# The scan stage of a hybrid decoder trunk: ScalarE in place of VectorE copies the corner product of each inverse out of PSUM

## What is computed

```
def step(state, inp):
    rt, wt, kt, vt, kkt, at = inp
    sa = jnp.einsum('bhij,bhj->bhi', state, -kkt)
    state = (state * wt[:, :, None, :] + sa[..., None] * (kkt * at)[:, :, None, :]
             + vt[..., None] * kt[:, :, None, :])
    return state, jnp.einsum('bhij,bhj->bhi', state, rt)
```

## Time and profile before

| | us |
|---|---|
| median of 3 runs | 3130.48 |
| lowest and highest | 3129.78 and 3132.05 |
| the profiled execution | 3130.32 |
| its span in the trace | 3128.5 |

### The profile page before, as it was taken

How to read it: one execution, slowest core, us unless ns; L and a number is a source line. 1 busy time by engine, 2 the same in 40 slices (tenths; PEclk the granted TensorE clock), 3 DMA queues, 4 the chain that set the end, 5 groups by cost and what they waited for, 6 DMA issues and landing times. The chain is left out here.

```text
span 3128.5 us, 52347 instructions
## 1 busy us (share of the span) xinstructions
PE 3056.2 (98%) x21306; PEld 2537.1 (81%) x21306; DVE 2147.3 (69%) x3225; ACT 1334.0 (43%) x2110; POOL 436.2 (14%) x570
## 2 busy tenths in 40 slices
PE   8999999899999999999999999999999999999998
PEld 6778777788988888778888788888888887888887
DVE  6777685677765677445444777777877777787786
ACT  6757566555545221033333333333433333444443
POOL 4334342655510011000000000000000000000000
PEclk9999999999999999999999999999999999999999
DMA  6466554322101644311111433333333334777873
GB/s 216 148 189 195 168 183 135 106 71 83 64 26 55 229 159 154 117 41 61 67 61 56 145 116 112 111 108 128 119 115 117 108 135 142 254 223 214 252 220 121
DMA packets 200092, 416.43 MB, mean 133 GB/s; under 512 B 15296, under 2 KB 99648, under 8 KB 193600
## 3 DMA queue, kind: packets, MB, share of 16 engines
q1 hardware_dynamic: 199872, 413.34, 39.9%
HBM read 295.82 MB, written 117.46 MB: 132 GB/s over the span
## 5 line engine op out<-in xcount | busy, mean ns | idle before, releaser
L3202 PE MATMUL ffn_ps<-ffn_t_p,ffn_w_p 128*128 128x512 f32 x2640 | 606.1, 389 | 0.0
L3202 PEld LDWEIGHTS ffn_ps<-ffn_t_p,ffn_w_p 128*128 128x128 f32 x2640 | 495.3, 188 | 103.4 <-DVE ffn_w_p L3377 0.6
L3217 PE MATMUL ffn_ps<-ffn_t_p_parts 128*128 128x512 f32 x1416 | 330.7, 393 | 5.8 <-DVE ffn_t_p_parts L3519 5.8
L3217 PEld LDWEIGHTS ffn_ps<-ffn_t_p_parts 128*128 128x128 f32 x1416 | 268.9, 190 | 62.8 <-DVE ffn_t_p_parts L3519 6.6
L431 POOL TENSOR_TENSOR w_low<-w_ring,w_high 128x1024 fp32r<-128x1024 f32 x84 | 215.2, 2564 | 313.1 <-ACT w_high L586 313.1
L3228 ACT ACTIVATE ffn_w_p<-ffn_w_p_sums 128x512 fp32r<-128x512 f32 x132 | 83.4, 632 | 335.7 <-DVE ffn_w_p_sums L3398 335.4
L547 PE MATMUL proj<-hn_high,w_high 128*128 128x512 f32 x544 | 222.0, 416 | 1.7 <-ACT hn_high L576 1.6
L547 PE MATMUL proj<-hn_high,w_low 128*128 128x512 f32 x544 | 209.6, 394 | 0.0
L547 PE MATMUL proj<-hn_low,w_high 128*128 128x512 f32 x544 | 207.9, 391 | 0.0
L3217 PE MATMUL ffn_ps<-ffn_t_p 128*128 128x512 f32 x696 | 162.5, 389 | 0.0
L3298 ACT ACTIVATE ffn_t_p_parts<-ffn_ring 128x1536 fp32r<-128x1536 f32 x59 | 87.7, 1487 | 159.9 <-PE ffn_ps L3217 156.3
(11 more groups left out here) (577 smaller groups left out, 6673.3 us busy)
## 6 DMA issues: line engine op xcount, KB each, us to landing
ffn_ring<-in_w_up SPq DMA_DIRECT2D x44, 1024.0 KB, 5.3
ffn_ring<-in_w_down SPq DMA_DIRECT2D x88, 512.0 KB, 5.4
w_ring<-in_w_feat SPq DMA_DIRECT2D x84, 512.0 KB, 4.0
ffn_ring<-scratch_values SPq DMA_DIRECT2D x88, 257.0 KB, 4.5
scratch_gates<-ffn_gate SPq DMA_DIRECT2D x44, 512.0 KB, 2.6
ffn_ring<-scratch_gates SPq DMA_DIRECT2D x88, 256.0 KB, 3.8
scratch_values<-ffn_raw SPq DMA_DIRECT2D x22, 513.0 KB, 3.5
scratch_values<-ffn_raw SPq DMA_DIRECT2D x22, 512.0 KB, 3.4
```

The lines of the kernel that those rows point to most:

```text
L3202: mm = pe.matmul(bank(name, s), w_part(name, a)[:, k * P:(k + 1) * P], t_part(name, b)[:, k * TB:(k + 1) * TB], start=k == a == b == 0, st ...
L3217: mm = pe.matmul(ps[:, DOWN_BANKS[2 * t + c]], down_part(n, x)[:, HID + t * TC:HID + (t + 1) * TC], down_part(n, y)[:, c * DH:(c + 1) * DH ...
```

## The change

The copy `corner_products(n)` moves from VectorE's queue to ScalarE's. In an iteration with a late chunk, VectorE goes from `prepare_kr` directly to `corner_scores(n)`. ScalarE does the copy after `level_out(m, 1)` and before `corner_inverse_out(n)`. What it reads and writes, and the semaphores that it waits for and signals, are the same; the form of the instruction on ScalarE is an activation with the function Copy.

```
@@ in the queue of ScalarE
+            def corner_products(n):
+                act.wait_ge(*cy_done.at(n))
+                act.activation(corner_y[HD:].rearrange("p h n -> p (h n)"), ps_g[HD:, n % 2, SIDES[0]], ACT.Copy).then_inc(cy_out.sem, 1)
+
             def corner_inverse_out(n):
                 act.wait_ge(*cx_done.at(n))
@@ its run(i)
                 if early:
                     level_out(m, 1)
                 if late:
+                    corner_products(n)
                     corner_inverse_out(n)
                     diagonal(n, 0, inv_out)
@@ in the queue of VectorE
-            def corner_products(n):
-                dve.wait_ge(*cy_done.at(n))
-                dve.tensor_copy(corner_y[HD:].rearrange("p h n -> p (h n)"), ps_g[HD:, n % 2, SIDES[0]]).then_inc(cy_out.sem, 1)
@@ its run(i)
                 if late:
-                    corner_products(n)
                     corner_scores(n)
                     picks_last(n)
```

## The result

| | before | changed |
|---|---|---|
| median, us | 3130.97 | 3137.88 |
| lowest and highest | 3127.52 and 3136.06 | 3134.75 and 3140.57 |
| runs | 18 | 18 |
| the profiled execution | 3130.32 | 3136.44 |
| its span | 3128.5 | 3134.7 |

The changed kernel is 0.19% slower by the ratio in the table, 5.9 us with an interval of 4 to 8; the two medians of the table lie 6.9 us apart. The forecast was 3133.6 us in a range of 3130.2 to 3136.0: the direction was right, the time lies outside the range. Single runs of either kernel spread over 6 to 9 us, so times are compared over many runs.

The account below looks back on a forecast made before the run. The prediction took TensorE's own queue as the bound of a usual iteration. Lateness of 14 x 0.20 = 2.8, plus 0.05 and 0.33, made 3.2 us, on 3130.4 giving 3133.6 us, range 3130.2 to 3136.0.

Parts of the forecast that it names:

- TensorE's queue sets the pace, VectorE waits: Usual iteration of the scan, 20.9 us: TensorE's own queue bounds it, VectorE waits before the copy, its relief gains nothing.
- The rival of VectorE's relief: Where TensorE waits for `kc`, each wait shrinks by 0.46 us, 2.8 us in six, giving 3130.8 us; chance 0.04.
- The copy takes 0.38 us, the release 0.05: Corner copy on ScalarE: length 0.38 us, as L1260, then 0.05 us from its end to the start of `corner_inverse`.
- It starts 0.50 us after `level_out`: ScalarE, usual chunk: corner copy overlaps `level_out`, starting 0.50 us after its start, so TensorE waits 0.20 us.
- no overlap at all: High end for a usual chunk: corner copy starts only when `level_out` (0.62 us) ends, making `corner_inverse` 0.32 us late.
- The last chunk, 0.48 us after `oy`: Last chunk, without `level_out`: copy starts 0.48 us after `oy`, `corner_inverse` is 0.58 us late, `rhs` 0.33 us later.
- The delay passes on 1:1: After `corner_inverse`: `off_times` and all later waits move with the delay, so each chunk's 0.20 us counts in full.
- the absorbed rival: In the scan, the delay meets waits that start elsewhere: 0 to 1 us, 3130.4 to 3131.4 us; chance 0.12.
- The sum: Over the scan's 16 chunks: 14 x 0.20 = 2.8, plus 0.05 for chunk 0 and 0.33 for the last, 3.2 us.
- The slower rival: Before `corner_inverse`: no overlap, 0.32 us, plus a TensorE restart of 0.14 a chunk, 7.0 us, 3137.4 us; chance 0.09.
- The clock: TensorE's half-clock dip after a long wait: one dip removed or added, at most 1.7 us, 3131.9 or 3135.3; chance 0.07.

Follow-up runs that it names:

- the wide copy: The changed kernel with ScalarE's corner copy over all 128 partitions in place of 64 to 127: 3133.72 us, 1.0006 of the kernel before.

## Why the prediction was wrong

- **TensorE's queue sets the pace, VectorE waits.** Right at the place of the change, not everywhere. VectorE's idle time before `factor` went from 0.39 to 1.11 us, forecast about 1, and nothing came back from its 16 missing copies. The rival of VectorE's relief falls: TensorE's six waits for `kc` went from 6.1 us only to 5.7. But "no matmul waits for a result of VectorE" was read off a list that can't show such a wait under matmuls still counted as busy: in every usual chunk L1614 was held up by VectorE's `start_inverse`, by up to 0.17 us. It follows the wait for `off_times`, so the lateness still passed through, and the relief could not reach it.
- **The copy takes 0.38 us, the release 0.05.** Right, 0.379 and 0.05. The corner copy on ScalarE is the shorter one (0.38 against 0.43 us), and it made no gain, since its place outweighed it.
- **It starts 0.50 us after `level_out`.** This is the step that failed. It took 0.64. The overlaps used were those between copies that all begin at partition 0; the corner copy begins at partition 64. The bound "no overlap at all", 0.32 us, was near but still short of the 0.34 measured, as it left out a gap of 0.02. A pair that matched in the first partitions was at hand in the trace of before, 734.29 - 733.88 = 0.41 us. The page ScalarE: Activation LUTs of the Trainium skill, section What ACT_TABLE_LOAD costs, gives 0.093 us of overlap: the trace agrees roughly, with 0.10 to 0.15, where the first partition stays, and disagrees where it changes. Its result, 0.23 us, fell short for the same reason as mine.
- **The last chunk, 0.48 us after `oy`.** The same error: 0.63. `rhs` became 0.48 us later, forecast 0.33.
- **The delay passes on 1:1.** Right in the usual chunks: the pitch rose from 20.68 to 21.04 us, which is the 0.34 and 0.02 that `start_inverse` takes more (0.65 for 0.63); over the six iterations that the prediction named it rose from 20.92 to 21.24, forecast 20.9 to 21.1. In two of the iterations nothing was added: from chunk 13 to 14 (24.68 before, 24.66 after) the longest wait for `kc` shrank from 2.28 to 1.88 us, and from 8 to 9 (21.77 and 21.78) the idle time without a releaser from 0.85 to 0.51. In some others more than 0.34 was added (0.51 from chunk 3 to 4). So the absorbed rival holds for about 0.7 us and falls for the rest, and that the sum comes out is in part luck. The prediction had no term for an instruction of VectorE whose length depends on where GpSimd stands; in the wide copy that term gives back a third of the lateness.
- **The sum.** With the measured term it is 14 x 0.34 + 0.19 for chunk 0 (0.05 + 0.14) + 0.48 = 5.4 us in place of 3.2. The trace has 5.15 us in the scan; chunk 0's part lies ahead of it and was absorbed there, which leaves 5.2 of the sum. That makes 3135.8 us of the forecast: the mis-sized term alone would have left it inside the range. Of the 4.3 us between 3133.6 and 3137.88, 2.2 are this term and 0.6 the base (the median of before was 3130.97 over 18 runs, not the 3130.4 taken), and with these two it is 3136.4. The lower clock is 0.5 to 1 us, by the groups of equal clock. Some 0.5 to 1 us is left without a cause, below what the intervals resolve: they allow 4 to 8 us for the change, and 5.4 lies within.
- **The slower rival** had nearly the right time, 3137.4, for half a reason, so the number was luck. Its missing overlap was there, in every chunk. Its second half, a restart of TensorE for 0.14 us, was not: `corner_inverse` takes 0.68 us after the wait as without it, and the next group follows at the old distance.
- **The clock** was a rival with either sign, and the one stretch more ahead of chunk 0 has its size: some 1.4 us, of which 0.81 are left by the start of the scan. Whether the change caused it is open.

The high end of the range came from the high end of the per-chunk bound and from one dip, never from both, and the base was taken without its own spread. So a miss of 0.14 us a chunk used up the room above the forecast, and 0.6 us in the base carried the time over the edge.

## What to carry to other kernels

An instruction moved to another engine starts where that engine's queue lets it, so its start is read from a pair of neighbours in the trace that match in their first partitions too, not in length alone. Where a step on the bound engine's path has 0.12 us of slack, put the copy ahead of the longer one, or give the bound engine other work first: here the second way gained 0.15%, where the bare move lost 0.19%. A list of waits with nothing in it is not yet a proof: compare the start of the matmul with the end of what feeds it. And a length of scan is compared only after the stretches at half clock in both traces are found. If the same instruction has two durations in a trace, look at what the other engines did at that moment before its length goes into a sum.

## What the runs showed of the hardware

- ScalarE: two activations in a row overlap by 0.10 to 0.15 us if both begin at the same partition (0.28 us apart for 64x256 at 0 and 0 or at 64 and 64, 0.47 to 0.50 after a 128x512). If the first partition changes, up or down, they don't, and 0.02 to 0.03 us are added (0.40, 0.41, 0.64). The comparison seems to be with the last activation that read the same memory, SBUF or PSUM: `level_out` and an exponential, both from partition 0, stood 0.62 us apart when the last read of SBUF had begun at partition 64, and 0.47 when it had begun at 0.
- VectorE and GpSimd: a masked copy from SBUF to SBUF takes 0.42 to 0.45 us alone and 0.49 to 0.74 beside GpSimd, whose own instruction goes from 0.40 to 0.58.
- TensorE: two 64x64 groups, `corner_inverse` and `off_times`, run interleaved when they stand next to each other. The order 64x128, 64x64, 64x128, 64x64 takes 1.90 us to the start of its last group, the order 64x128, 64x128, 64x64, 64x64 takes 1.38.
- TensorE's clock: the same program had a mean granted clock of 0.994 to 0.997 from run to run, and 0.001 went with some 1.3 us of 3130. A stretch of 3.4 us at 0.50 cost 1.5 us where a wait of 2.28 us lies in front of it (24.68 for 23.19).
